# Retention's input projection: fifteen block products over three token tiles in ten chunks, in place of one plain tile and Strassen's seven products on the other two

## The reference, cut to what matters

```python
# h: (384 tokens, 1024); in_w: (1024, 8192)
q, k, v, g_f, g_b = jnp.split(h @ in_w, SPLIT1, axis=-1)   # widths 1024, 1024, 2048, 2048, 2048
q, k = apply_grid_rope(q), apply_grid_rope(k) * 128 ** -0.5  # latent tokens only get the rotary
y_f, y_b = retention(q, k, v, forward), retention(q, k, v, backward)   # 8 heads, chunks of 128 tokens
mixed = silu(g_f) * head_rms(y_f) + silu(g_b) * head_rms(y_b)
out = mixed @ out_w                                        # (2048, 1024)
```

## Time and profile before

| what | value |
|---|---|
| runs | 1314.14, 1313.4, 1319.27 us; median 1314.14 |
| profiled execution | 1314.11 us, span 1312.2 us |
| busy share | PE 93%, PEld 51%, DVE 39%, ACT 22%, POOL 10% |
| granted TensorE clock, mean | 0.988 |

### The profile page before, as it was taken

How to read it: one execution, slowest core, us unless ns; L and a number is a source line. 1 busy time by engine, 2 the same in 40 slices (tenths; PEclk the granted TensorE clock), 3 DMA queues, 4 the chain that set the end, 5 groups by cost and what they waited for, 6 DMA issues and landing times. The chain is left out here.

```text
span 1312.2 us, 14335 instructions
## 1 busy us (share of the span) xinstructions
PE 1226.2 (93%) x5590; PEld 664.3 (51%) x5590; DVE 509.8 (39%) x1010; ACT 291.2 (22%) x700; POOL 134.9 (10%) x145
## 2 busy tenths in 40 slices
PE   7999989998999987989999999999999989999786
PEld 3543446445344423345777756766776453444232
DVE  1375575143000002644525546545565560000044
ACT  2122244132111111124112212311222241111112
POOL 0079800000000010001101000001000000000100
PEclk9999999998999999999999999999999999999998
DMA  9859995485999995732413223231234959999995
GB/s 384 352 204 390 392 424 234 192 346 205 427 427 427 427 427 222 297 130 80 155 70 111 106 81 112 97 136 73 80 145 170 413 202 425 427 426 428 427 424 207
DMA packets 37170, 351.09 MB, mean 268 GB/s; under 512 B 4128, under 2 KB 9568, under 8 KB 17248
## 3 DMA queue, kind: packets, MB, share of 16 engines
q1 hardware_dynamic: 23760, 315.89, 58.6%
q0 software_dynamic: 5472, 20.97, 4.0%
q10 hardware_dynamic: 7856, 13.14, 2.7%
HBM read 331.35 MB, written 18.64 MB: 267 GB/s over the span
## 5 line engine op out<-in xcount | busy, mean ns | idle before, releaser
L668 PE MATMUL PS<-ring,hT 128*128 128x512 f32 x432 | 190.4, 594 | 0.8 <-ACT hT L1280 0.8
L899 PE MATMUL PS<-ring,hT 128*64 128x512 f32 x720 | 163.5, 604 | 20.1 <-DMA ring<-moe_w_up 14.8
L668 PEld LDWEIGHTS PS<-ring,hT 128*128 128x128 f32 x432 | 81.0, 190 | 99.1 <-issue 98.3
L899 PEld LDWEIGHTS PS<-ring,hT 128*64 128x64 f32 x720 | 51.9, 139 | 128.8 <-issue 99.0
L1117 PE MATMUL PS<-ring 128*128 128x256 f32 x480 | 108.7, 379 | 1.2 <-ACT ring L1576 1.2
L2130 DVE TENSOR_TENSOR area<-area,PS 128x512 f32<-128x512 f32 x16 | 11.0, 687 | 234.3 <-PE PS L899 234.3
L919 PE MATMUL PS<-ring,area 128*64 128x512 f32 x400 | 91.4, 605 | 7.8 <-DMA ring<-moe_w_down 6.2
L1117 PEld LDWEIGHTS PS<-ring 128*128 128x128 f32 x480 | 91.1, 190 | 13.9 <-issue 1.6
L1098 PE MATMUL PS<-ring,area 128*128 128x512 f32 x192 | 83.8, 593 | 3.8 <-ACT area L1661 3.8
L1117 PE MATMUL PS<-ring,hT 128*128 128x256 f32 x360 | 82.6, 379 | 0.0
L1117 PEld LDWEIGHTS PS<-ring,hT 128*128 128x128 f32 x360 | 68.2, 190 | 13.4 <-issue 4.8
(11 more groups left out here) (311 smaller groups left out, 1437.0 us busy)
## 6 DMA issues: line engine op xcount, KB each, us to landing
ring<-moe_w_down SPq DMA_DIRECT2D x25, 2048.0 KB, 25.1
ring<-mod_w SPq DMA_DIRECT2D x24, 2048.0 KB, 11.7
ring<-moe_w_gate SPq DMA_DIRECT2D x23, 2048.0 KB, 22.3
ring<-moe_w_up SPq DMA_DIRECT2D x22, 2048.0 KB, 24.2
ring<-in_w SPq DMA_DIRECT2D x20, 2048.0 KB, 7.6
area<-moe_w_up SPq DMA_DIRECT2D x8, 2048.0 KB, 20.8
ring<-out_w SPq DMA_DIRECT2D x7, 2048.0 KB, 9.1
area<-moe_w_down SPq DMA_DIRECT2D x7, 2048.0 KB, 30.6
```

Of the source, the lines that this page charges most:

```text
L668: mm = pe.matmul(out, lhs(k), rhs(k), start=k == 0, stop=k == KD - 1)
L899: mm = pe.matmul(PS[64 * e:64 * e + 64, j, :], gT[:, 4 * half + k, 64 * e:64 * e + 64], w[e][k], start=half == 0 and k == 0, stop=half == ...
```

## The change

Chunk `q0` stays as it was. The other 15 steps (7680 columns) become 10 chunks of three blocks of 256 columns (`CHUNKS`), 3 MB each; one block is one head's v or gate, or two heads' q or k. Activations (3 tiles x 2 halves of channels) times weights (2 halves x 3 blocks) is done by 15 products, each of 4 matmuls of 256 columns; a plain scheme has 18. A chunk is eight `part` events on TensorE of two products each (the last has one).

Per chunk VectorE makes 11 weight sums of 1024 elements (`terms_ahead`: 5 before the chunk starts; `terms`: 6 within it, some of them in place in the ring) and 19 additions of products (`add_products`: 17 of 256 elements, 2 of 512). ScalarE makes 14 copies of 256. Eleven activation sums are made once. Nothing on PE's side is left of the plain tile 0 but in `q0`. Silu is applied once per head on 3x2x256 elements (before: per step on 1024 and 512).

The order of events is written anew. VectorE and ScalarE have lists of their own, derived from it (`plan_vector`, `plan_scalar`). On VectorE the first four sums ahead of chunk c stand behind part 6 of chunk c-1 and the fifth behind its part 7; where outs come before the chunk, behind the outs' fifth and sixth. Of the sums within, one stands at part 1, two at part 3 (behind product 6), two at part 4, one at part 5. The rotary stands at the end of the chunk that completes k or q of four heads. On ScalarE B of a head stands behind the next part or out, and silu of a head two steps behind the chunk that made its gates. Slot 2 takes the last third of each chunk (its halves alternate), slots 4 and 5 hold `x_sum`, `k1T` and copied products, the spare slot `qtok` and `v1`. The MoE weights of layer 1 for slots 2 and 4 wait for the last product. The host orders the weight into `in_c1`. The diff, cut:

```diff
+CHUNKS = ((("k", 0), ("k", 1), ("v", 0)), (("f", 0), ("b", 0), ("v", 1)), (("f", 1), ("b", 1), ("v", 2)),
+          (("f", 2), ("b", 2), ("v", 3)), (("f", 3), ("b", 3), ("q", 2)), (("q", 3), ("k", 2), ("k", 3)),
+          *((("v", a), ("f", a), ("b", a)) for a in range(4, RH)))
+TERMS_BY = {4: 2, 5: 3, 6: 4, 7: 5, 8: 7, 9: 8, 10: 9, 11: 1, 12: 10, 13: 6, 14: 11}
+NPROD, NTERM, NCOPY, NADD, NUSE = 15, 11, 14, 19, 8
 def plan_retention():
...
+    e = [("job", "q0", t) for t in range(TT)] + part(0, 0, 3) + [("gate", 0, 0)] + part(0, 3)
+    e += part(1, 0, 4) + [("turn", 0, 0)] + part(1, 4, 6) + [("A", 0, 0)] + part(1, 6)
+    for c in (2, 3):
+        e += part(c, 0, 1) + [("B", c - 2, 0)] + part(c, 1, 5) + [("C", c - 2, 0), ("A", c - 1, 0)] + part(c, 5)
+    e += outs(0, 0, 2) + [("B", 2, 0)] + outs(0, 2, 5) + [("A", 3, 0)] + outs(0, 5, 6) + [("C", 2, 0)]
+    e += part(4, 0, 1) + [("B", 3, 0)] + part(4, 1)
+    e += part(5, 0, 4) + [("C", 3, 0)] + part(5, 4)
+    e += part(6, 0, 4) + [("turn", 1, 0)] + part(6, 4)
+    e += outs(1, 0, 2) + [("A", 4, 0)] + outs(1, 2, 4) + [("B", 4, 0)] + outs(1, 4, 6)
+    e += part(7, 0, 1) + [("C", 4, 0)] + part(7, 1)
+    e += part(8, 0, 1) + [("A", 5, 0)] + part(8, 1, 4) + [("B", 5, 0)] + part(8, 4)
+    e += part(9, 0, 1) + [("C", 5, 0), ("A", 6, 0)] + part(9, 1, 4) + [("B", 6, 0)] + part(9, 4)
+    e += [("A", 7, 0)] + outs(2, 0, 3) + [("B", 7, 0)] + outs(2, 3, 6)
...
+def plan_vector():
+    for a, ev in enumerate((("part", 2, 4), ("part", 3, 4), ("out", 0, 5), ("part", 5, 3), ("part", 7, 0), ("part", 9, 0),
+                            ("out", 2, 0))):
+        moved(order, ("C", a, 0), ev)
...
+            def product(c, m):
...
                 for k in range(4):
+                    mm = pe.matmul(product_of(c, m), lhs[:, k, :], rhs[:, k, :], start=k == 0, stop=k == 3)
...
+            def terms(c, piece):
...
+                elif piece == 3:
+                    dve.wait_ge(prod_mm, NPROD * c + 6)
+                    w_add(term[:, 0], w01, w11, ALU.subtract)
+                    dve.wait_ge(term_ready, NTERM * c + 6)
+                    w_add(term[:, 2], w02, w11, ALU.subtract)
+                elif piece == 4:
...
+            def add_products(c, piece):
+                if piece == 0:
+                    dve.wait_ge(prod_copied, NCOPY * c + 5)
...
+                elif piece == 2:
+                    dve.wait_ge(prod_copied, NCOPY * c + 11)
+                    onto(y[2][:, 2, :], copied[0], ALU.add, 1)
+                    onto(y[0][:, 1:3, :], copied[0].unsqueeze(1).to_broadcast([P, 2, HALF]), ALU.subtract, 2)
+                    onto(y[2][:, 2, :], copied[1], ALU.add, 4)
+                    onto(y[0][:, 0, :], copied[1], ALU.add, 2)
...
+            for ev in VECTOR:
+                if kind == "part":
+                    if b:
+                        terms(a, b)
+                        add_products(a, b - 1)
+                elif kind == "ahead":
+                    terms_ahead(a, b)
+                elif kind == "end":
+                    add_products(a, NUSE - 1)
...
```

More of the change, by code:

```diff
@@ L77, in plan_retention, with part @@
+X_SUMS = ("A3", "A6", "A12", "A13", "A2", "A8", "A10", "A5", "A15", "A9", "A1")
+PRODUCTS = (
[4 rows of a table added]
+TERMS_BY = {4: 2, 5: 3, 6: 4, 7: 5, 8: 7, 9: 8, 10: 9, 11: 1, 12: 10, 13: 6, 14: 11}
+NPROD, NTERM, NCOPY, NADD, NUSE = 15, 11, 14, 19, 8
 def plan_retention():
-    def jobs(*steps):
-        return [("job", s, t) for s in steps for t in range(TT)]
+    def part(c, a=0, b=NUSE):
+        return [("part", c, i) for i in range(a, b)]
     def outs(j, a, b):
         return [("out", j, i) for i in range(a, b)]
-    e = jobs("q0", "k0") + [("gate", 0, 0)] + jobs("v0") + [("turn", 0, 0)] + jobs("f0", "b0")
@@ L169, in plan_stream @@
     for kind, step, _ in RET:
-        key = ("in", 1, step) if kind == "job" else ("out", 1, step) if kind == "out" else None
+        key = ("in", 1, step) if kind in ("job", "part") else ("out", 1, step) if kind == "out" else None
         if key and key not in seen:
@@ L179 @@
 INDEX = {key: i for i, key in enumerate(STREAM)}
-USES = [sum(PLACE[j] == PLACE[i] for j in range(i)) for i in range(len(STREAM))]
+IS_CHUNK = [kind == "in" and l == 1 and c != "q0" for kind, l, c in STREAM]
+LOADED = [sum(32 if PLACE[j] in (APART, ONCE) or IS_CHUNK[j] else 16 for j in range(i + 1) if PLACE[j] == PLACE[i])
+          for i in range(len(STREAM))]
 BEFORE = [max([j for j in range(i) if PLACE[j] == PLACE[i]], default=None) for i in range(len(STREAM))]
@@ L187 @@
         JOBS[(0, _c, _t)] = len(JOBS) + 1
-for _kind, _s, _t in RET:
-    if _kind == "job":
-        JOBS[(1, _s, _t)] = len(JOBS) + 1
+for _t in range(TT):
+    JOBS[(1, "q0", _t)] = len(JOBS) + 1
 JOBS0 = 2 * CB + 3 * TT
@@ L262, with moved @@
 ROPE_NO = {e: n + 1 for n, e in enumerate(ROPES)}
-ROPED = {e: sum(r in RET[:RET.index(e)] for r in ROPES) for e in OUT_EVENTS}
-LAST_JOB = JOBS[(1,) + JOB_EVENTS[-1][1:]]
-def backbone_kernel(nc, x_in, cst, par, fgain, cache_k, cache_v, st_in, mod_w, in_w, out_w, w_gate,
+TURNED_IN = (MADE_IN[("k", 1)], MADE_IN[("k", 3)])
+def moved(order, ev, before):
+    order.remove(ev)
+    order.insert(order.index(before), ev)
+def plan_vector():
+    order = list(RET)
+    for a, ev in enumerate((("part", 2, 4), ("part", 3, 4), ("out", 0, 5), ("part", 5, 3), ("part", 7, 0), ("part", 9, 0),
+                            ("out", 2, 0))):
+        moved(order, ("C", a, 0), ev)
+    for c in range(NCHUNK):
+        order.insert(order.index(("part", c, NUSE - 1)) + 1, ("end", c, 0))
+        if c:
+            before = RET[RET.index(("part", c, 0)) - 1]
+            if before == ("part", c - 1, NUSE - 1):
+                order.insert(order.index(("part", c - 1, NUSE - 2)) + 1, ("ahead", c, 0))
+                order.insert(order.index(("part", c - 1, NUSE - 1)) + 1, ("ahead", c, 1))
+            else:
+                j = max(e[1] for e in RET[:RET.index(("part", c, 0))] if e[0] == "out")
+                order.insert(order.index(("out", j, 4)) + 1, ("ahead", c, 0))
+                order.insert(order.index(("out", j, 5)) + 1, ("ahead", c, 1))
+    return order
@@ new lines, in plan_scalar @@
+def plan_scalar():
+    order = list(RET)
+    steps = [e for e in RET if e[0] in ("part", "out")]
+    for a in range(RH):
+        after = next(e for e in RET[RET.index(("B", a, 0)):] if e in steps)
+        order.remove(("B", a, 0))
+        order.insert(order.index(after) + 1, ("B", a, 0))
+        c = MADE_IN[("b", a)]
+        after = steps[steps.index(("part", c, NUSE - 1)) + 2]
+        order.insert(order.index(after) + 1, ("silu", a, 0))
+    return order
+VECTOR, SCALAR = plan_vector(), plan_scalar()
@@ L268, in backbone_kernel @@
+ROPED = {}
+for _ev in OUT_EVENTS:
+    _ends = [e[1] for e in VECTOR[:VECTOR.index(_ev)] if e[0] == "end"]
+    ROPED[_ev] = 2 + 2 * (TURNED_IN[0] in _ends) + 4 * (TURNED_IN[1] in _ends)
+def backbone_kernel(nc, x_in, cst, par, fgain, cache_k, cache_v, st_in, mod_w, in_w, in_c, out_w, w_gate,
                     w_up, w_down, y_out, new_k, new_v, st_out):
@@ L547, in _ @@
                     if PLACE[i] == TERMS and l == 1 and kind == "out":
-                        sp.wait_ge(proj_mm, LAST_JOB)
+                        sp.wait_ge(prod_mm, NPROD * NCHUNK)
                     fill(i, src)
+                    if IS_CHUNK[i]:
+                        if c < 2:
+                            released(sp, max(j for j in range(i) if PLACE[j] == SHARE))
+                        o = 2 * BLOCK if PLACE[i] else 0
+                        sp.dma_start(slot(SHARE)[:, o:o + 2 * BLOCK], in_c[c][:, SLOT:SLOT + 2 * BLOCK]
+                                     ).then_inc(ring_loaded[PLACE[i]], 16)
                 else:
@@ L1124, in _ @@
                     bank_free(n)
[L1125 to L1145, removed]
+                if kind == "part":
+                    if b == 0:
+                        arrived(pe, INDEX[("in", 1, a)])
+                    bank_free(UNTIL[("use", a, b)])
+                    for m in range(2 * b, min(2 * b + 2, NPROD)):
+                        product(a, m)
                 elif kind == "job":
@@ new lines, in terms_ahead @@
+            def terms_ahead(c, n):
+                (w00, w01, w02), (w10, w11, w12) = ([w_part(c, k, j) for j in range(3)] for k in range(2))
+                if n == 0:
+                    arrived(dve, INDEX[("in", 1, c)])
+                    need(dve, prod_mm, NPROD * (c - 1) + 12 if c else 0)
+                    w_add(term[:, 1], w10, w12, ALU.add)
+                    w_add(term[:, 0], w00, w10, ALU.subtract)
+                    dve.wait_ge(term_ready, NTERM * c + 1)
+                    w_add(term[:, 2], term[:, 1], w00, ALU.subtract)
+                    dve.wait_ge(term_ready, NTERM * c + 2)
+                    w_add(w10, w10, w11, ALU.add)
+                else:
+                    dve.wait_ge(term_ready, NTERM * c + 3)
```

(25 more changed lines are left out.)

348 lines of the change are left out of this document (182 added, 166 removed), and 4 rows, old and new, of the table PRODUCTS.

## The result

The changed kernel takes 1320.21 us (median of 20 runs, 1318.05 to 1326.05) against 1313.95 us for the kernel before in the same comparison; the ratio is 1.0051, 95% interval 1.0041 to 1.0062. It is slower by about 6 us, where 9 were forecast. The measured time lies inside the forecast's own range, 1316 to 1331.

A forecast was written before the change was run, and what follows sets the result against it. TensorE was taken to bound the projection stage. -25.4 saved, -3.1 old waits, +29.2 new waits and +8.5 slow clock gave +9.2 us, so 1323.3 us; likeliest case 1316 to 1331, range for all 1290 to 1335.

The forecast's parts named there:

- TensorE's saving, 25.4 us: Projection stage: fifteen removed steps take 284.2 us, ten new chunks 258.8, so TensorE saves 25.4 us.
- 3.1 of old waits: Projection stage: two TensorE waits of the old order, 1.23 and 1.91 us, have no counterpart, 3.1 us more saved.
- Waits, 29.2 us: Projection stage: TensorE waits for five late C's and for sums in chunks 5 and 6, 29.2 us together.
- the 1.3 in chunk 6: Chunk 6: four rotaries on VectorE stand ahead of sums that products 8 and 10 need, 1.3 us of waiting.
- The clock, 8.5 us: Behind the five waits longer than 2.42 us TensorE runs at the 1.2 GHz level, 1.7 us each, 8.5 together.
- The table load: ScalarE's silu table load taken as 1.28 us from the row, without the skill's 1.38 us more for draining.
- everything behind the stage at nothing: Behind the projection stage: earlier first MoE transfer and unchanged tail were costed at nothing.
- A: Rival, chance 0.28: the waits hide and TensorE's saving stays, 1285.6 us at best, 1305 with half the waits.
- B: Rival, chance 0.17: waits as worked out but the clock unharmed, 1314.8 us.
- C: Rival, chance 0.10: VectorE sets the pace, the seven waits grow by some 2 us each, +14, 1337 us.

The follow-up runs named there:

- the last experiment: Changed kernel with silu one step earlier and late C's further back on TensorE, C0 and C1 also later on VectorE, C2 a part before B3: 1285.24 us, 0.9796.
- the silu run: Changed kernel with ScalarE doing each head's silu one step earlier: 1309.87 us, 0.9962 of the kernel before.
- the sums on an eighth: Changed kernel with VectorE's eleven weight sums per chunk made on 128 of 1024 elements: 1335.57 us, total unusable as expert choice changed; stage 402.6 us.
- The idle matmuls: Changed kernel with idle 256-column matmuls on TensorE just ahead of C0, C1, C2, C4 and C5: 1312.36 us, 0.9985 of the kernel before.
- the three with C later: Changed kernel with late C's further back on TensorE: alone 1294.91 us; with silu one step earlier 1290.82; with that and C0, C1 later on VectorE 1285.24.
- C later: Changed kernel with each late C one to two parts further back on TensorE, silu unchanged: 1294.91 us, 0.9859 of the kernel before.

## Why the prediction was right

**TensorE's saving, 25.4 us and 3.1 of old waits: right.** The 1200 narrow records run at 3.45 us per 16, and the last experiment, in which nothing is left in the way, has a stage shorter by 28.3 us than before; 28.5 were worked out.

**Waits, 29.2 us: the mechanism right, the size 4 too high.** Counted from start to start, as the prediction did, they are 3.8, 3.8, 5.8, 5.6 and 4.5 for the five C's (forecast 4.2, 4.2, 6.2, 5.9, 5.1) and 1.9 for chunk 5 (2.3); the 1.3 in chunk 6 didn't come. That is 25.4. In chunk 5 half of it stood ahead of C3 itself (0.9 us) and not, as forecast, all of it ahead of the two sums behind it. The links of the chains were a little cheaper: four sums 4.55 us (4.75), A and C 5.3 (5.7). Which link ends last was right in each: ScalarE's copies for C0 and C1 (the silu run moves these two pauses, the sums on an eighth don't), VectorE's own list for C2, C4 and C5 (the reverse).

**The clock, 8.5 us: right.** The idle matmuls give 8.7 back. The stretches behind the five pauses cost 1.6, 1.7, 2.4, 1.6 and 1.4 us. The single row it rested on proved less than it seemed: in the changed kernel's trace the same instructions of the last expert wait 2.42 us again (1267.09), and the sixteen records behind take 3.65 us, the full-clock figure. The pauses forecast were all longer, and all five were followed by a fall. What the prediction took from the Trainium skill, "TensorE: Matmul & The Clock Gate", section "Part 1: The HAM clock gate", that activity releases the slow state, agrees with these runs: TensorE kept at work in the same waits stays at 1.00.

**The table load: the row was right, and the rule did not hold here.** The Trainium skill, "ScalarE: Activation LUTs", section "What ACT_TABLE_LOAD costs", adds 1.38 us of draining to a switch of tables. It shows in neither load of the chain above: each begins within 0.02 us of the end of the instruction before it, and the next starts as closely behind it.

**The sum in the stage.** -25.4 - 3.1 + 25.4 + 8.7 = +5.6, where the stage grew by 4.8; the 0.8 between them was not traced to a row. The forecast was +9.2: the waits were 3.8 shorter than worked out, the clock cost 0.2 more.

**Behind the stage, not predicted.** The profiled span grew by 6.6 us, 1.8 more than the stage. The prediction had put everything behind the stage at nothing, so these 1.8 us bring the total closer to the forecast by luck. From the end of the output projection to the experts' transposes the changed kernel takes 0.7 us more, and these transposes 8.49 us where the kernel before took 5.60. It is the clock once more, in the run of short matmuls and waits with which the experts start:

```profile
1063.41 2.25 PE L916 MATMUL PS<-hT,V 128*32 128x384 f32 x16 [0.68 <-ACT hT L1356]
```

The same line takes 1.50 us in the run with idle matmuls, at full clock. Between here and the experts the clock falls in five of the eight profiled executions (after, silu earlier and the three with C later) and stays up in the other three, with the same waits ahead (2.0 us ahead of a transpose, at 1060.26 here). The experts' transposes take 7.2 to 8.5 us in three of the five and 5.60 in the rest. What decides it was not tried. Only about 2 of the 3.6 us reach the end of the execution; that the experts' weight stream hides the rest was not shown.

**The rivals.** A (the waits hide) was wrong for this kernel but names what the last experiment made: 1285.6 was its best case, 1285.2 was measured. (Its upper end, 1305 "with half the waits and no clock loss", is a slip: its own sum gives 1300.) B is out by the idle matmuls. C is out by the sums on an eighth and by the last run, in which VectorE works 290 of 358 us and delays nothing. In "C later" its kind of wait, on a weight sum, did come, by an order and not by the load.

## What to carry to other kernels

A saving in the bounding engine has to be read together with the order of the two engines that feed it: VectorE had a quarter of its time free, and ScalarE almost three quarters, and still TensorE was held back five times, three times by VectorE's own order and twice by ScalarE's, because the awaited instruction stood behind work that nobody was waiting for yet. For each point where the bounding engine waits, add up what stands ahead of the awaited instruction in its own engine's list since the last common event; here the rows of the old profile were enough to find all five, and moving the wait one or two pieces later added no work. Then follow what stood behind the moved piece as well.

## What the runs showed of the hardware

A pause can cost more than its length. In the stage every pause of 2.56 us or more (twelve, in four runs) was followed by a stretch at the 1.2 GHz level worth about 1.4 to 2.9 us, and none of 1.65 or less was. At 1.97 us it went both ways in one execution: C4 in the run with sums on an eighth has it (its transposes take 1.43), C2, with the same idle time, has not (0.88). Outside the stage longer ones went both ways too. The first line here is the changed kernel's, to be held against the earlier trace rows; the second, from the run with sums on an eighth, follows 3.15 us of waiting in layer 0's experts, and its clock is 1.00:

```profile
1267.09 3.65 PE L1001 MATMUL PS<-ring,area 128*64 128x512 f32 x16 [2.42 <-DMA ring<-moe_w_down]
```

```profile
480.14 3.65 PE L981 MATMUL PS<-ring,hT 128*64 128x512 f32 x16 [3.15 <-DMA ring<-moe_w_up]
```

So a pause between 1.97 and 3.15 us may or may not be followed by a fall. Each of the ten of 3.61 us or more in the stage was. Matmuls whose result is thrown away, in the pauses alone, gave back 8.7 us. Two kernels with the same instructions up to layer 1 reach `q0` up to 9 us apart, so a single total says less than a stage.
